# Forgetting attention's decay products: plain 32-bit operands straight from the scan's buffer instead of a high and a low part in the single-pass format

## The reference, cut to what matters

```python
log_f = jax.nn.log_sigmoid(f_logit + b_f)
cum = jnp.cumsum(log_f, axis=1)
...
logits = jnp.einsum('bqhd,bkhd->bhqk', q_blk, k) * (dh ** -0.5)
decay = c_blk[..., None] - cum_t[:, :, None, :]
p = jax.nn.softmax(jnp.where(causal, logits + decay, NEG_INF), axis=-1)
```

## Time and profile before

| what | value |
|---|---|
| median of 3 runs | 3246.19 us |
| lowest and highest run | 3244.92 and 3250.03 us |
| span of the profiled execution | 3250.2 us |
| PE busy | 3225.4 us (99%) |
| PE weight loads busy | 3038.7 us (93%) |
| DVE busy | 2563.3 us (79%) |
| ACT busy | 1519.1 us (47%) |
| POOL busy | 1101.5 us (34%) |
| TensorE clock granted, mean | 0.999 |

### The profile page before, as it was taken

One profiled execution on the slowest core, in us unless ns is written; L12 is line 12 of the kernel. 1 busy time (PEld: TensorE's weight loads), 2 busy tenths in 40 slices (PEclk: granted clock), 3 DMA queues, 4 the chain that ended last, 5 costly groups with the idle time before them and its releaser, 6 DMA issues. The chain is left out here.

```text
span 3250.2 us, 55293 instructions
## 1 busy us (share of the span) xinstructions
PE 3225.4 (99%) x19718; PEld 3038.7 (93%) x19718; DVE 2563.3 (79%) x4920; ACT 1519.1 (47%) x2310; POOL 1101.5 (34%) x713
## 2 busy tenths in 40 slices
PE   8999999999999999999999999999999999999998
PEld 8878888999999999999988788889999999999998
DVE  6654349999997899999866543599999878999998
ACT  5553233477773333333355533334777733333333
POOL 1000014334345555555300000242343366555552
PEclk9999999999999999999999999999999999999999
DMA  4214322589999999999721143235999999999996
GB/s 148 77 53 143 142 94 87 192 321 381 381 379 409 412 400 409 404 407 411 285 91 66 66 146 140 85 113 181 356 380 379 379 404 419 401 402 406 401 405 255
DMA packets 230931, 894.78 MB, mean 275 GB/s; under 512 B 22784, under 2 KB 67984, under 8 KB 182912
## 3 DMA queue, kind: packets, MB, share of 16 engines
q1 hardware_dynamic: 116944, 465.34, 37.7%
q0 software_dynamic: 93008, 337.91, 26.6%
q10 hardware_dynamic: 20832, 89.74, 6.8%
HBM read 801.42 MB, written 91.49 MB: 275 GB/s over the span
## 5 line engine op out<-in xcount | busy, mean ns | idle before, releaser
L1402 PE MATMUL bank<-xT_hi,hi 128*128 128x352 f32 (+1 forms) x2688 | 926.6, 345 | 1.9 <-DVE xT_lo L951 1.7
L901 DVE TENSOR_TENSOR lo<-raw,hi 128x2048 fp32r<-128x2048 f32 (+2 forms) x320 | 699.9, 2187 | 278.6 <-ACT hi L552 269.6
L1404 PE MATMUL bank<-xT_hi,lo 128*128 128x352 f32 (+1 forms) x2688 | 910.6, 339 | 0.0
L1403 PE MATMUL bank<-xT_lo,hi 128*128 128x352 f32 (+1 forms) x2688 | 910.5, 339 | 0.0
L552 ACT ACTIVATE hi<-raw 128x2048 fp32r<-128x2048 f32 (+2 forms) x338 | 620.4, 1835 | 373.6 <-PE bank L1404 333.0
L1404 PE MATMUL bank<-w_hi,lo 128*128 128x352 f32 x2048 | 662.4, 323 | 0.0
L1402 PE MATMUL bank<-w_hi,hi 128*128 128x352 f32 x2048 | 661.2, 323 | 0.7 <-DVE w_lo L1320 0.6
L1403 PE MATMUL bank<-w_lo,hi 128*128 128x352 f32 x2048 | 658.1, 321 | 0.0
L541 POOL DMA_INDIRECT rows<-in_v_rows,ids x256 | 417.4, 1630 | 350.8 <-DVE h L1292 276.3
L1402 PEld LDWEIGHTS bank<-xT_hi,hi 128*128 128x128 f32 x2688 | 506.0, 188 | 31.9 <-issue 5.7
L1404 PEld LDWEIGHTS bank<-xT_hi,lo 128*128 128x128 f32 x2688 | 505.4, 188 | 25.4
(11 more groups left out here) (232 smaller groups left out, 4192.3 us busy)
## 6 DMA issues: line engine op xcount, KB each, us to landing
raw<-in_stream SPq DMA_DIRECT2D x352, 1024.0 KB
gate_d<-gate_s ACTq DMA_DIRECT2D x22, 2048.0 KB
act_d<-act_s ACTq DMA_DIRECT2D x120, 352.0 KB
act_in<-act_d SPq DMA_DIRECT2D x120, 352.0 KB
gate_in<-gate_d SPq DMA_DIRECT2D x96, 384.0 KB
gate_in<-gate_d SPq DMA_DIRECT2D x32, 256.0 KB
rows<-in_u_rows,ids POOLq DMA_INDIRECT x256
rows<-in_v_rows,ids POOLq DMA_INDIRECT x256
```

The source lines that it names most:

```text
L901: dve.tensor_tensor(lo[s][:, 0:n], raw[s][:, 0:n], hi[s][:, 0:n].bitcast(F32), ALU.subtract).then_inc(lo_done, 1)
L1402: pe.matmul(dst, a_[0], b_[0], start=first, stop=False)
L1403: pe.matmul(dst, a_[0], b_[1], start=False, stop=False)
L1404: return pe.matmul(dst, a_[1], b_[0], start=False, stop=last)
```

## The change

The decay product takes its moving operand from `fg[:, 1]`, where the scan leaves the sums, and its stationary operand from a plain 32-bit `select` with one row per head. With that the tile `cum`, ACT's copy into it, DVE's overwrite, the tile `select_in` with its copy, and the multiplier column go away. The tile `fg` keeps the room of `cum` in front of it, so that nothing else in on-chip memory moves. PE waits for the scan (`f_link`) where it waited for `cum_lo`. The order of all other instructions stays on every engine.

```diff
-        select = sb("select_sb", [P, 2 * P], F32R)
+        select = sb("select_sb", [P, 2 * P])
...
-        cum = sb("cum", [F_ROWS, T], F32R, heads)
-        fg = sb("fg", [F_ROWS, 2, T], to=heads)
+        fg = sb("fg", [F_ROWS, 3, T], to=heads)[:, 1:]
...
-        first_loads = [(pos_i, a["pos"]), (sin, a["inv_freq"]), (select_in, a["select"])]
+        first_loads = [(pos_i, a["pos"]), (sin, a["inv_freq"]), (select, a["select"])]
...
-                 (bgate, a["bgate"]), (bforget, a["bforget"]), (sink, a["sink"]),
+                 (bgate, a["bgate"]), (bforget[:, 0:DEPTH], a["bforget"]), (sink, a["sink"]),
...
                     act.wait_ge(first_in, 16 * len(first_loads))
-                    act.activation(select[:], select_in[:], ACT.Copy)
                     act.wait_ge(angle_ready, 1)
...
                         for tt in range(NT):
-                            if c == 3 and tt == NT - 1:
-                                act.wait_ge(f_link, 4 * l + 4)
-                                act.activation(cum[:], fg[:, 1], ACT.Copy).then_inc(cum_hi, 1)
                             proj_evict(l * HP, c // 2, tt, True)
...
-                dve.wait_ge(cum_hi, l + 1)
-                dve.scalar_tensor_tensor(out=cum[:], in0=cum[:].bitcast(F32), scalar=bforget[:, DEPTH:DEPTH + 1], in1=fg[:, 1],
-                                         op0=ALU.mult, op1=ALU.add).then_inc(cum_lo, 1)
...
                         if w == FIRST_OF[2]:
-                            pe.wait_ge(cum_lo, l + 1)
+                            pe.wait_ge(f_link, 4 * l + 4)
...
-                                done = pe.matmul(dst[hh], select[of, hp:hp + 1].broadcast_to([F_HALF, P]), cum[of, keys],
+                                done = pe.matmul(dst[hh], select[of, hp:hp + 1].broadcast_to([F_HALF, P]), fg[of, 1, keys],
                                                  start=False, stop=True)
...
-        select[[row, row + 2], x // 2] = -1.0 / SCALE
+        select[row, x // 2] = -1.0 / SCALE
```

More of the change, by code:

```diff
@@ L315, in build @@
         mixer.close()
-        start = ExitStack()
-        select_in = sb("select_in", [P, 2 * P], to=start)
-        start.close()
         idx1T, idx2T = sb("idx1T", [P, TD]), sb("idx2T", [P, TD])
@@ L373, in build @@
             sem(n) for n in ("proj_ps", "proj_ev", "rope_link", "heads_ps", "heads_act", "heads_dve"))
-        f_copied, f_ps, f_x, f_act, f_link, cum_hi, cum_lo = (
-            sem(n) for n in ("f_copied", "f_ps", "f_x", "f_act", "f_link", "cum_hi", "cum_lo"))
+        f_copied, f_ps, f_x, f_act, f_link = (sem(n) for n in ("f_copied", "f_ps", "f_x", "f_act", "f_link"))
         s_ps, mx_link, lg_done, ex_done, den_link, pn_done, tr_done, pt_done, pv_done, o_hi, o_lo = (
@@ L1862, in layout @@
     norms = np.stack([norm1_g, norm2_g], axis=1).reshape(2 * depth, NK, P)
[L1863 to L1867, removed]
+    forget = np.tile(b_forget.reshape(depth, HP, 2).transpose(1, 2, 0), (1, 2, 1))
+    forget = np.tile(forget.reshape(F_COLS, depth), (F_REPS, 1))
+    forget = np.concatenate([forget, np.zeros((DH - F_HALF, depth), np.float32), forget])
     out = {
```

## The result

The changed kernel takes 3254.48 us (median of 11 runs, 3252.74 to 3260.39), the kernel before 3246.19 us (median of 11 runs, 3243.67 to 3250.03): 8.3 us more. The ratio is 1.0025 with a 95% interval of 1.0017 to 1.0033, so +5.5 to +10.7 us. That is slower, clear of no change, and small.

A forecast was written before the change was run, and what follows sets the result against it. PE was taken to bound the kernel, busy 3225.4 of 3250.2 us and hardly waiting in attention. Plain products +8.9 us and the layer starts -0.1 us gave +8.8 on 3246.2, so 3255.0 us, range 3251.0 to 3259.0.

The forecast's parts named there:

- PE sets the pace in attention: Attention passes: PE hardly ever waits, only 0.7 us for DVE's scaling, so work added to PE moves all that follows.
- The plain products cost their columns: Decay pairs in branch B: 0.21 us per 128 columns, 2.10 instead of 0.62 us per pass, +8.9 us in all.
- The steps: Branch B's steps 5, 6 and 7 of the first pass: expected at about 1.5, 1.5 and 1.9 us.
- The weight loads cost nothing: Each plain product loads weights twice, costed at nothing because the product running before them covers the loads.
- The start of the layer, -0.1 us: Before each layer's first pass: dropping ACT's copy and DVE's overwrite wins 0.05 us each, at most 0.46 us in all.
- The rival built on it: Not slower: the scan, copy, overwrite chain sets the first pass's pace; 2.8 us won, 3243.4 us; chance 0.04.
- The sum: Whole kernel: +8.9 us for plain products less 0.1 us at the layer starts, +8.8 us.
- Two issues, two columns' worth: Rival on decay products: each of two issues costs what a single-pass product does; 3249.8 us; chance 0.07.
- loads in the open: Rival: plain weight loads uncovered, 96 of 0.186 us add 17.9 us on top, 3272.9 us; chance 0.03.
- a fixed price per pair: Rival: each decay pair also costs a fixed 0.22 us, 24 times; +14.1 us, 3260.3 us; chance 0.06.
- slack in a later stage: Sign against the forecast: passes grow by 4.4 us per layer but the time does not, so a later stage has slack.

The follow-up runs named there:

- e5: The changed kernel with every decay product issued twice, on half the factor in select: 3270.86 us, ratio 1.0063 against the kernel before.
- e6: The changed kernel with decay products on 12 partitions per head instead of 60: 3264.14 us, ratio 1.0043 against the kernel before.
- e3: The kernel before, still single-pass products, but the scan writes straight into the single-pass tile, without copy and overwrite: 3250.12 us, ratio 1.0002.
- e2: The kernel before with only the decay products' format made plain; copy, overwrite and both parts stay: 3258.45 us, ratio 1.0029.
- e1: The changed kernel measured and profiled again with no edit: 3257.54 us, ratio 1.0032 against the kernel before.

## Why the prediction was right

The time, 3254.48 us, lies 0.5 us from the predicted 3255.0 and inside the range. That it came so close is luck: the medians of the kernel before in the three sets of runs are 3246.19, 3248.73 and 3250.43 us, and the prediction was built on the first. What bears the mechanism out are the passes, 9.1 us longer where 8.8 were forecast. Point by point:

- *PE sets the pace in attention.* Shown: leaving the products out shortens the passes by 13.1 us, issuing them twice lengthens them by 13.0 us, and PE's waits for DVE's scaling stay at 0.7 us.
- *The plain products cost their columns.* Predicted 1.48 us more per pass, measured 1.53. The slope of 0.21 us per 128 columns was right (e5: 0.85 us for 512). Both terms came out a little larger than they were read from single steps with two decimals: the plain products 2.16 us per pass (2.10 taken), the single-pass ones 0.64 (0.62 taken). The steps came out at 1.51, 1.49 and 1.92 us where 1.5, 1.5 and 1.9 were expected.
- *The weight loads cost nothing.* Right, with the cover that was named: in the changed kernel the first loads stand 0.42 us ahead of their products, beside the product before them. In e6, where they do not, 0.2 us are lost; whether the late load or the change of rows itself takes them was not told apart.
- *The start of the layer, -0.1 us.* 0.05 us was taken for each layer; e3 shows about 0.1 us in the first and nothing beyond the scatter in the second. The rival built on it is refuted by e2 and e3.
- *The sum.* 9.2 - 0.1 = 9.1 us, the 9.1 us of the passes. The medians say 8.3 and, in e1, 8.8, and the intervals of the two ratios include 9.1.
- *Two issues, two columns' worth* and *loads in the open* are refuted by the steps above, *a fixed price per pair* by e5. That last rival gave as its reason that the rows are 60 and not 64, which is not enough of a difference; with 12 rows a price of this size is there, at every change of rows.
- What the prediction had no place for is the pace of the values' stage. It had asked to look for slack in a later stage if the passes grew and the time did not, and by the two spans that seemed to be so. It was the pace.

## What to carry to other kernels

Where PE never waits, the price of a product is what lies between the start of it and the start of the next, in a place with and in a place without it; a record of 797 ns stood here for 0.23 us of PE's time. A high and a low part stacked on unused partitions of one single-pass product did for 0.64 us per pass what plain products do for 2.16, and their making cost 0.1 us in the whole program, because it lay beside PE's work. Before two profiles are compared by their spans, compare stages that the change does not touch: here they differed by more than the change.

## What was not expected of the hardware

A stage of nothing but equal products ran for most of its length at one of a few paces, 158.9, 160.0 or 161.1 ns for 352 columns, with PE busy throughout and the same granted clock of 1.00, and one program took different ones in different executions, once two within one stage. In the ten profiles the stage lasted between 489 and 495 us in a layer. That fits the 6 to 12 us by which runs of one kernel differ in a set; only profiles show the pace, so it is not shown for the unprofiled runs. What sets it was not tried and stays open.
